# Query up-projection of a latent attention: six weight tiles for eight, and the rotation of all heads at once

## The reference, cut to what matters

```
q = jnp.einsum('bsr,rhd->bshd', rms_norm(c_q_raw, q_norm_g), w_uq)   # r = 384, h = 8 heads, d = 64 + 32
q_nope = q[..., :64]
q_rope = apply_rope(q[..., 64:], cos, sin)      # pairs channel i with i + 16, of 32
s = einsum(q_nope, k_nope) + einsum(q_rope, k_rope)   # all heads share k_rope
def apply_rope(x, cos, sin):
    x1, x2 = x[..., :half], x[..., half:]
    return concatenate([x1 * cos - x2 * sin, x2 * cos + x1 * sin], axis=-1)
```

## Time and profile before

| | |
|---|---|
| median of 3 runs | 1838.35 us (1838.19 to 1838.78) |
| the profiled execution's own time | 1839.44 us |
| its span, first to last instruction | 1838.1 us |
| PE busy | 1823.1 us, 99% |
| DVE busy, ACT busy | 1374.2 us (75%), 1040.7 us (57%) |
| granted TensorE clock, mean | 0.999 |
| memory traffic | 199 GB/s mean |

### The profile page before, as it was taken

The page is one execution under the profiler, slowest core; times in us unless marked ns, Lnnn a source line. Parts: engine busy times, 40 slices in busy tenths (PEclk is TensorE's granted clock), DMA queues, the critical chain, the costliest instruction groups (busy, mean ns, idle before and its releaser), DMA issues.

```text
span 1838.1 us, 36166 instructions
## 1 busy us (share of the span) xinstructions
PE 1823.1 (99%) x15117; PEld 1790.8 (97%) x15117; DVE 1374.2 (75%) x2388; ACT 1040.7 (57%) x1690; POOL 3.1 (0%) x9
## 2 busy tenths in 40 slices
PE   9999999999999999999999999999999999999998
PEld 9999999999999999999899999999999999999998
DVE  7787786677876788768667887797877559778754
ACT  6444665665444544466656554676665457666633
POOL 0000000000000000000000000000000000000000
PEclk9999999999999999999999999999999999999999
DMA  8876332357784677533246776454555554455553
GB/s 302 295 283 229 131 138 93 138 192 260 266 297 174 229 264 283 209 138 139 97 163 237 283 295 245 146 184 143 181 183 186 190 177 170 159 179 189 184 184 115
DMA packets 52386, 365.31 MB, mean 199 GB/s; under 512 B 6684, under 2 KB 7356, under 8 KB 10880
## 3 DMA queue, kind: packets, MB, share of 16 engines
q1 hardware_dynamic: 51792, 362.22, 54.6%
q10 hardware_dynamic: 432, 0.79, 0.1%
HBM read 361.93 MB, written 1.05 MB: 197 GB/s over the span
## 4 chain that ended last, share of the span: by engine, by line
PE 88%; DVE 9%; ACT 1%; DMA 1%; issue 1%; SPq 0%; DVEq 0%; ACTq 0%
PE bank L561 26%; PE bank L563 26%; PE bank L562 26%; DVE w_lo L1746 3%; PE bank L621 2%; PE bank L617 1%; PE bank L618 1%; DMA ada_raw<-in_ada_w 1%; PE bank L848 1%; PE bank L863 1%; PE bank L893 0%; DVE s_pool L2266 0%; PE bank L800 0%; DVE ada_raw L1892 0%; ACT w_hi L1197 0%
## 5 line engine op out<-in xcount | busy, mean ns | idle before, releaser
L561 PE MATMUL bank<-xn_hi,w_hi 128*128 128x272 f32 (+2 forms) x2640 | 758.3, 287 | 0.0
L563 PE MATMUL bank<-xn_lo,w_hi 128*128 128x272 f32 (+2 forms) x2640 | 749.0, 284 | 0.0
L562 PE MATMUL bank<-xn_hi,w_lo 128*128 128x272 f32 (+2 forms) x2640 | 748.9, 284 | 0.0
L561 PEld LDWEIGHTS bank<-xn_hi,w_hi 128*128 128x128 f32 x2640 | 498.2, 189 | 6.9 <-issue 4.0
L562 PEld LDWEIGHTS bank<-xn_hi,w_lo 128*128 128x128 f32 x2640 | 498.2, 189 | 0.9
L563 PEld LDWEIGHTS bank<-xn_lo,w_hi 128*128 128x128 f32 x2640 | 498.2, 189 | 0.0
L1197 ACT ACTIVATE w_hi<-raw_a 128x1024 fp32r<-128x1024 f32 (+2 forms) x278 | 303.2, 1091 | 276.6 <-PE bank L563 242.7
L1197 ACT ACTIVATE w_hi<-raw_b 128x1024 fp32r<-128x1024 f32 (+2 forms) x280 | 305.7, 1092 | 266.3 <-PE bank L563 240.8
L1746 DVE TENSOR_TENSOR w_lo<-raw_b,w_hi 128x1024 fp32r<-128x1024 f32 (+2 forms) x280 | 354.2, 1265 | 130.1 <-ACT w_hi L1197 127.9
L1746 DVE TENSOR_TENSOR w_lo<-raw_a,w_hi 128x1024 fp32r<-128x1024 f32 (+1 forms) x276 | 350.2, 1270 | 121.5 <-ACT w_hi L1197 120.4
L561 PE MATMUL bank<-h_hi,w_hi 128*128 128x272 f32 (+1 forms) x704 | 200.8, 285 | 1.6 <-DVE full L1945 1.6
(11 more groups left out here) (361 smaller groups left out, 2660.0 us busy)
## 6 DMA issues: line engine op xcount, KB each, us to landing
raw_b<-in_weights SPq DMA_DIRECT2D x122, 1024.0 KB, 4.7
raw_a<-in_weights SPq DMA_DIRECT2D x121, 1024.0 KB, 4.7
ada_raw<-in_ada_w SPq DMA_DIRECT2D x48, 1024.0 KB, 4.8
raw_a<-in_weights SPq DMA_DIRECT2D x16, 1408.0 KB, 6.3
raw_b<-in_weights SPq DMA_DIRECT2D x16, 1408.0 KB, 5.8
c_rows<-in_c_rows SPq DMA_DIRECT2D x3, 512.0 KB, 5.6
raw_b<-in_weights SPq DMA_DIRECT2D x2, 768.0 KB, 4.1
raw_a<-in_weights SPq DMA_DIRECT2D x2, 640.0 KB, 3.7
```

The costliest lines, as they stand in the source:

```text
L561: pe.matmul(o, wh, xh, start=start, stop=False)
L562: pe.matmul(o, wl, xh, start=False, stop=False)
L563: return pe.matmul(o, wh, xl, start=False, stop=stop)
```

## The change

The columns of the query weights are put in another order, without the swapped copies: first the rotary columns of all eight heads (two tiles, four heads in each), then the plain ones (four tiles, two heads in each). That is six tiles with three k-tiles, in three units of 768 columns. Unit 12 now gives the rotary rows of all heads, in one bank with 128 partitions: 32 rows for each of four heads, and heads 4 to 7 in the second half. ACT copies it to SBUF (`q_rope`). DVE exchanges the partners with a shuffle across partitions, multiplies by sine and cosine, and adds: four instructions for all heads. ACT then puts the rotated rows in their place beside the plain ones, in four copies (`q_heads`), two at place 15 and two at place 16. The tables have to be there on all four groups of 32 partitions, which is eight small ACT instructions at the start for three.

```diff
-M2_UNITS = ([[1024, 1024]] * 2 + [[1024, 256]] + [[1024, 1024]] * 8 + [[1024, 512]] + [[1024, 1024]] * 12)
+M2_UNITS = ([[1024, 1024]] * 2 + [[1024, 256]] + [[1024, 1024]] * 3 + [[768, 768], [768, 1024]] + [[1024, 1024]] * 3 + [[1024, 512]] + [[1024, 1024]] * 12)
...
-QUERY_BANKS, KEY_BANKS, VALUE_BANKS = [0, 4, 5, 6], [1, 7], [2, 3]
+QUERY_BANKS, KEY_BANKS, VALUE_BANKS = [5, 0, 4], [1, 7], [2, 3]
...
# PE, before a score product
-                if h % 2 == 0:
-                    pe.wait_ge(*k.at("tile_a", ("q", l, h // 2)))
-                    pe.wait_ge(*k.at("att_v", ("qrope", l, h // 2)))
+                    pe.wait_ge(*k.at("att_a", ("qrope", l)))
+                if h % 4 == 0:
+                    pe.wait_ge(*k.at("tile_a", ("q", l, h // 4)))
...
# PE, the query projection
-        for i in range(8):
-            h, kk = divmod(8 * part + i, 3)
-            b, s = QUERY_BANKS[h // 2], slice(i * P, (i + 1) * P)
...
+        b = QUERY_BANKS[part]
+        take(b)
+        for i in range(6):
+            t, kk = divmod(i, 3)
+            s = slice(i * P, (i + 1) * P)
+            m = product(bank[b][:, N * t:N * t + N], wh[:, s], wl[:, s], c.cq_hi[:, kk, :], c.cq_lo[:, kk, :], kk == 0, kk == 2)
...
# ACT
+    def q_heads(l):
+        act.wait_ge(*k.at("att_v", ("qrope", l)))
+        for q in range(4):
+            act.activation(c.q_all[RP, q:q + 5:4, :], c.q_rope[ROPE * q:ROPE * q + ROPE, :, :], ACT.Copy).then_inc(
+                *k.up("att_a", ("qrope", l) if q == 3 else None))
+            if q == 1:
+                yield
...
-                  (6, 12, k_rope(l)), (9, 14, pooled(l)), (17, 35, attention2(l))]
+                  (6, 12, k_rope(l)), (9, 14, pooled(l)), (15, 17, q_heads(l)), (17, 35, attention2(l))]
...
+                    b = QUERY_BANKS[part]
+                    if part == 0:
+                        act.activation(c.q_rope, bank[b][:, :].rearrange("p (h n) -> p h n", h=2), ACT.Copy).then_inc(*k.up("att_a", ("q", l)))
+                        continue
+                    for j in range(2):
+                        h = 4 * (part - 1) + j
+                        act.activation(c.q_all[0:NOPE, h:h + 3:2, :], bank[b][NOPE * j:NOPE * j + NOPE, :].rearrange("p (h n) -> p h n", h=2),
+                                       ACT.Copy).then_inc(*k.up("tile_a", ("q", l, part - 1) if j else None))
...
# DVE
+        dve.wait_ge(*k.at("att_a", ("q", l)))
+        dve.stream_shuffle(r, q, PAIRS).then_inc(*k.up("att_v"))
         dve.wait_ge(*k.newest("att_v"))
+        dve.tensor_tensor(r, r, table(c.sin2), ALU.mult).then_inc(*k.up("att_v"))
+        yield
+        dve.tensor_tensor(q, q, table(c.cos2), ALU.mult).then_inc(*k.up("att_v"))
+        dve.wait_ge(*k.newest("att_v"))
+        dve.tensor_tensor(q, q, r, ALU.add).then_inc(*k.up("att_v", ("qrope", l)))
...
# the weights' columns
-        uq = np.concatenate([uq, uq[:, :, NOPE + swap]], axis=2).reshape(QL, MH * P)
+        uq = np.concatenate([uq[:, :, NOPE:].reshape(QL, MH * ROPE), uq[:, :, 0:NOPE].reshape(QL, MH * NOPE)], axis=1)
```

More of the change, by code:

```diff
@@ L241, in __init__ @@
         self.v2, self.gain = sb("v2", [P, L, V2_ALL]), sb("gain", [P, L, 2, KD])
-        self.cos2, self.sin2 = sb("cos2", [96, N]), sb("sin2", [P, N])
+        self.cos2, self.sin2 = sb("cos2", [P, N]), sb("sin2", [P, N])
         block_start = place
@@ L298, in __init__ @@
         self.gates2 = self.gates2_x[:, :, TN]
-        self.q_swap = self.gates2[:, 8:16, :]
+        self.q_rope, self.q_turned = self.gates2[:, 8:10, :], self.gates2[:, 10:12, :]
         self.u_pool, self.s_pool = sb("u_pool", [P, 4, T + 2]), sb("s_pool", [P, 2, T])
@@ L325 @@
 VALUE_TILE_BANKS = [0, 5, 0, 1]
-QUERY_BANKS, KEY_BANKS, VALUE_BANKS = [0, 4, 5, 6], [1, 7], [2, 3]
-PAIR_PART = [0, 1, 2, 2]
+QUERY_BANKS, KEY_BANKS, VALUE_BANKS = [5, 0, 4], [1, 7], [2, 3]
 def whole_tile(t):
@@ L1056, in queries @@
         pe.wait_ge(*k.at("x_lo", ("cq", l, 2)))
-        for i in range(8):
-            h, kk = divmod(8 * part + i, 3)
-            b, s = QUERY_BANKS[h // 2], slice(i * P, (i + 1) * P)
[L1060 to L1064, removed]
+        b = QUERY_BANKS[part]
[4 more added lines that the diff above has]
+            m = product(bank[b][:, N * t:N * t + N], wh[:, s], wl[:, s], c.cq_hi[:, kk, :], c.cq_lo[:, kk, :], kk == 0, kk == 2)
+        free[b] = [("tile_a", ("q", l, part - 1))] if part else [("att_a", ("q", l))]
         end_unit(u, m)
@@ L1318, in ffn @@
                     act.wait_ge(*k.at("rope_v", "angles"))
-                    for rows in (RS, RP):
+                    for q in range(4):
+                        rows = slice(ROPE * q, ROPE * q + ROPE)
                         act.activation(c.sin2[rows, :], c.angle[RP, :], ACT.Sin).then_inc(*k.up("rope_a"))
-                    act.activation(c.cos2[RP, :], c.rest[RP, :], ACT.Sin).then_inc(*k.up("rope_a", "sin"))
+                        act.activation(c.cos2[rows, :], c.rest[RP, :], ACT.Sin).then_inc(*k.up("rope_a", "sin" if q == 3 else None))
                 load_table(LN_EXP_SET)
@@ L2225, in k_rope, with q_rope, table @@
         yield
[L2227 to L2246, removed]
-        dve.wait_ge(*k.newest("att_v"))
-        dve.tensor_tensor(q, q, r, ALU.add).then_inc(*k.up("att_v", ("qrope", l, 3)))
+    def q_rope(l):
+        q, r = c.q_rope, c.q_turned
+        def table(t):
+            return t[:, :].unsqueeze(1).broadcast_to([P, 2, N])
+        dve.wait_ge(*k.at("att_a", ("q", l)))
+        dve.stream_shuffle(r, q, PAIRS).then_inc(*k.up("att_v"))
+        dve.wait_ge(*k.newest("att_v"))
+        dve.tensor_tensor(r, r, table(c.sin2), ALU.mult).then_inc(*k.up("att_v"))
[3 more added lines that the diff above has]
+        dve.tensor_tensor(q, q, r, ALU.add).then_inc(*k.up("att_v", ("qrope", l)))
     def pooled(l):
@@ L2309, in mixer2 @@
                   (3, 12, latent(l, "cq", 3, c.sq2[:, 0:N], [c.gate[:, 0, 0:N], c.gate[:, 1, 0:N]], c.cq, c.cq_hi, c.cq_lo, V_QG)),
-                  (6, 13, k_rope(l)), (8, 15, pooled(l)), (13, 26, q_rope(l, u0 + 12)), (17, 35, attention2(l))]
+                  (6, 13, k_rope(l)), (8, 15, pooled(l)), (13, 16, q_rope(l)), (17, 35, attention2(l))]
         u = u0
@@ L2557, in _layer2 @@
         w = i["w_in_2"][l]
-        swap = np.roll(np.arange(ROPE), ROPE // 2)
         uq = i["w_uq_2"][l].reshape(QL, MH, QK)
-        uq = np.concatenate([uq, uq[:, :, NOPE + swap]], axis=2).reshape(QL, MH * P)
+        uq = np.concatenate([uq[:, :, NOPE:].reshape(QL, MH * ROPE), uq[:, :, 0:NOPE].reshape(QL, MH * NOPE)], axis=1)
         kr = w[:, 1152:1184]
```

## The result

The changed kernel took 1849.26 us (median of 4, 1848.21 to 1855.33), the kernel before 1838.57 beside it (1838.19 to 1839.52): a ratio over all runs of 1.0064, with a 95% interval of 1.0051 to 1.0076 (by the medians alone 1.0058; the run of 1855.33 pulls the ratio up). By the medians it is 10.7 us slower. I had forecast 1843.3 us, 5.0 slower, with a range up to 1847.0, and the time lies above that.

What follows compares the result with a forecast made beforehand. PE was taken as the bound, busy 1823.1 of 1838.1 us. Per layer, a first score product 2.87 us late less 0.37 back gives 2.5; two layers add 5.0 to 1838.35: 1843.3 us, range 1840.5 to 1847.0.

Steps and rivals of the forecast that it cites:

- What goes: Query units: 18 products fewer per layer, 2.10 us of PE; DVE's low parts of units 12 to 14 each 0.27 us shorter.
- Steps 1 and 2: On DVE, unit 17's low part ends 1.53 us earlier than before, with the shuffle taken as 0.70 us.
- Step 3: Load of units 20 and 21: issued at once, used 4.57 us later, so ACT splits unit 20 from 1220.50.
- Step 4: ACT works without a gap from unit 20's split to the last rotated copy: 6.19 us, each copy 0.61.
- Step 5: PE waits 5.0 us at the first score product, which starts 2.87 us later than before in each layer.
- T0: At the start of the products with v, DVE is now in time with the probabilities, giving 0.37 us back per layer.
- S0 held by about 5 us at the full clock: The forecast itself: first score product waits for ACT's copies, clock unchanged; between 1842 and 1844.5 us, 55%.
- the fall of the clock: Rival: PE drops to 1.2 GHz in the wait, losing 1.75 us in a layer; 1845.1 or 1846.8 us, 20%.
- The rival on the other side: The first score product doesn't wait and PE's saving stands: 4.9 us less, 1833.4 us, 7%.

Runs made afterwards that it cites:

- e1: Changed kernel, but score products read zeros as q's rotary rows and don't wait for ACT's four copies, which are still made: 1838.85 us, ratio 1.0005 to the kernel before.
- e8: The changed kernel run again, unaltered, for a second profile and more times: 1849.20 us, ratio 1.0055 to the kernel before.
- e2: Changed kernel plus 40 unused products on PE just ahead of the first score product's wait: 1845.71 us, ratio 1.0027 to the kernel before.
- e4: Changed kernel, but the load of units 22 and 23 is issued only when that of 20 and 21 has landed: 1850.32 us, ratio 1.0056.
- e3: Changed kernel, but each of heads 0 to 3 waits for its own ACT copy instead of the last: 1839.43 us, ratio 0.9997 to the kernel before.
- e6: Changed kernel without ACT's copies: DVE's last addition writes four pieces straight into q, each head waiting for its own: 1834.68 us, ratio 0.9976 to the kernel before.
- e7: As e1, with ACT's four copies left out altogether: 1834.51 us, ratio 0.9978 to the kernel before.

## Why the prediction was wrong

*What goes.* Right in the products. 18 products a layer, 2.10 us (6.30 for 8.40), and a low part of 768 columns took the 0.95 us that I had put in. But I put PE's loss at unit 16 at nothing, and 0.2 us of the 2.10 were lost by S0: the values start 9.20 us from the first query product, not 9.10, and S0, when nothing holds it (e1), comes at 17.86, not at 17.66.

*Steps 1 and 2, DVE's chain.* Right within 0.2 us: shuffle 0.73 (I took 0.70), and SP could issue the load 11.69 us from the first query product where it was 13.39 before, 1.70 earlier instead of 1.53, since some neighbours on DVE overlap.

*Step 3, the load.* Mis-sized in one layer of the first trace: 5.60 us instead of 4.57, with an instruction transfer in it; in the second layer and in e8 it was 4.70 to 4.78.

*Step 4, ACT.* The order was right to the instruction. 6.46 us from unit 20's split to S0 instead of 6.19: a copy took 0.64, not 0.61, and S0 came 0.21 after the last one.

*Step 5.* S0 was to be 2.87 us late and was 3.99 and 3.21, in e8 3.18 and 3.10. The terms above are the difference. From S0 to T0 0.37 us were to come back; at the full clock (e2) it was 0.25.

*The rivals.* Here the prediction failed. Its sum put the products behind the wait at the full clock, that is at no cost, and they ran at a granted clock of 0.50. I took "S0 held by about 5 us at the full clock" for the likeliest and gave the fall of the clock 20%. It fell in every such wait that was traced: in both layers of the first trace, of e4 and of e8, and in e3 after 2.27 us. (In the second layer of the first trace it fell only as S0 began, 5 us after the last product.) With it the sum would have been 5.0 + 2 x 1.75 = 8.5 us at my own price, 1846.8. The price was low too in two of the three traces: 1.6 and 1.5 us in the first, 2.1 to 2.9 in e8 and e4. Of the 5.4 us between the 10.4 of the spans and my 5.0, 3.2 are the clock, 1.5 are S0's lateness beyond 2.87, and 0.7 lie outside the stage.

The Trainium skill (TensorE: Matmul & The Clock Gate, "What's actually happening"), which I had set beside this rival, has the array fall to 1.2 GHz after it has been idle, and so spoke for it. The trace agrees: 0.50 behind waits of 5.73 and 4.90 us. I held the absence of such a gap in the trace of before against it, which is no evidence: a trace without long waits can't show what a long wait does. Nor are the first microseconds the place of its longest gap, as I wrote; that is a wait of 1.2 us for DVE near 1121 us, behind which the clock stayed at 1.00.

*T0.* That DVE would be in time at T0 was right only because S0 was held; in e1, where it isn't, T0 waits 1.67 and 1.59 us. The rival on the other side, in which PE's saving stands when S0 waits for nothing, had 1833.4 as its price. e1 is that case, and gave nothing: the same four copies delayed the first exponential, and T0. I had followed the copies to the one instruction that waits for them by name, and not to what is queued behind them on ACT. Only with the copies off ACT (e6, e7) does most of that gain come: 1834.7 and 1834.5, which is 4.0 and 4.2 us less than the kernel before where the price was 4.9.

## What to carry to other kernels

Work that moves from one engine to another arrives at a place in that engine's queue: read what stands ahead of it there, above all a split of weights that waits for a load, and what stands behind it, and who waits for each. Count a wait of the matmul engine of some microseconds as the wait and the slow products behind it; here 1.5 to 2.9 us came on top of waits of 4.4 to 5.7 us, and 1.45 on top of one of 2.27. When an edit costs an engine that is the bound nothing by itself, look for the idle place in the other queues before choosing where the new work goes: the same rows written in four pieces by DVE where it was idle (e6), instead of in one piece and then copied four times by ACT, were worth 14.5 us (e8 against e6).

## What the runs showed of the hardware that I had not expected

The granted clock was 0.54 on average over 3.6 us behind a wait of 2.27 us (e3), and 1.00 behind waits of 1.42 us (e3) and 1.67 (e1); forty useless products in the wait kept it at 1.00 (e2). The 1.67 us are no safe length: two of e1's ten executions, of 1842.97 and 1845.14 us, show a mean clock of 0.997, lower than any of the 23 executions of the kernel before beside them, and there is no trace of these two.

The load of one megabyte took 4.57 to 4.83 us from issue to use where ACT was free to take it, and 5.38 to 5.74 where a 16 KB instruction transfer ran in its first half. Where that transfer falls differs between executions of one kernel.

On ACT, copies of 32 partitions that write with a stride into another group of partitions followed each other without overlap, 0.63 us long and 0.65 from start to start, where a copy of 128 x 512 on the same engine let the next instruction begin after 0.47 (1209.96 to 1210.43 in the changed kernel). The copies of the plain rows, 64 x 512, show it too: they start 0.48 us apart in the kernel before, where two heads are written side by side (L1655, 1215.71 us), and 0.62 apart in the changed one, where the heads are written with a stride (L1663, 1215.51 us).
